# The first block's attention with transposed scores, a row-maximum pass and the softmax's sums out of the value product

## The reference, cut to what matters

```
# kind 0, window: tokens within 128 positions, all 256 context tokens, and a sink logit per head
s_loc = einsum(q, k) * 64**-0.5, masked where |qpos - kpos| > 128
s_ctx = einsum(q, k_ctx) * 64**-0.5
p = softmax(concat[s_loc, s_ctx, sink])          # the sink takes weight, but has no value
o = p_loc @ v + p_ctx @ v_ctx
# kind 1, global: 512 tokens and 256 context tokens
p = softmax(einsum(q, [k, k_ctx]) * 64**-0.5);  o = p @ [v, v_ctx]
# layer 0 only: the 256 context queries, over the 256 context keys, both kinds (kind 0 with the sink)
```

## Time and profile before

| | |
|---|---|
| median of 3 runs | 3906.89 us (3906.81 to 3909.35) |
| the profiled execution's own time | 3902.73 us |
| its span | 3900.9 us |
| TensorE busy | 3302.3 us, 85% |
| VectorE busy | 1055.7 us, 27% |
| ScalarE busy | 659.3 us, 17% |
| GpSimd busy | 440.3 us, 11% |
| mean granted clock of TensorE | 0.86 |

### The profile page before, as it was taken

The page is one execution under the profiler, slowest core; times in us unless marked ns, Lnnn a source line. Parts: engine busy times, 40 slices in busy tenths (PEclk is TensorE's granted clock), DMA queues, the critical chain, the costliest instruction groups (busy, mean ns, idle before and its releaser), DMA issues. The chain is left out here.

```text
span 3900.9 us, 41076 instructions
## 1 busy us (share of the span) xinstructions
PE 3302.3 (85%) x16972; PEld 1921.7 (49%) x16972; DVE 1055.7 (27%) x2000; ACT 659.3 (17%) x1275; POOL 440.3 (11%) x636
## 2 busy tenths in 40 slices
PE   3799998479999938999758777479998998879997
PEld 0456773323333303577332111168785586748875
DVE  0225542321111122443130000132324266222232
ACT  0111120100000111111100000032222155122231
POOL 1006700011111110170001111100000000000000
PEclk7896558589999968855869999889999979989998
DMA  9131000369999891100249999912312100132130
GB/s 393 39 97 44 1 0 11 140 234 389 385 388 391 308 374 54 65 1 1 78 172 413 414 412 412 371 54 87 108 58 97 65 1 1 65 113 87 65 119 27
DMA packets 141428, 637.02 MB, mean 163 GB/s; under 512 B 11824, under 2 KB 19008, under 8 KB 86000
## 3 DMA queue, kind: packets, MB, share of 16 engines
q1 hardware_dynamic: 121104, 575.58, 37.4%
q0 software_dynamic: 20192, 59.58, 5.0%
HBM read 611.95 MB, written 23.17 MB: 163 GB/s over the span
## 5 line engine op out<-in xcount | busy, mean ns | idle before, releaser
L897 PE MATMUL bank<-slots,HT 128*32 128x512 f32 x4096 | 479.1, 600 | 79.3 <-DMA slots<-in_w_up_dram 41.5
L667 PE MATMUL bank<-slots,HT 128*128 128x512 f32 (+2 forms) x960 | 400.7, 578 | 20.4 <-ACT done_mark L1531 20.4
L897 PEld LDWEIGHTS bank<-slots,HT 128*32 128x32 f32 x4096 | 121.7, 110 | 400.8 <-issue 243.4
L667 PEld LDWEIGHTS bank<-slots,HT 128*128 128x128 f32 x960 | 182.4, 192 | 230.3 <-issue 204.5
L667 PE MATMUL bank<-hT_high,chunk_high 128*128 128x512 f32 x704 | 277.3, 394 | 8.3 <-DVE low_slots L1922 8.3
L667 PE MATMUL bank<-hT_high,low_slots 128*128 128x512 f32 x704 | 277.7, 395 | 0.0
L667 PE MATMUL bank<-hT_low,chunk_high 128*128 128x512 f32 x704 | 276.9, 393 | 0.0
L916 PE MATMUL bank<-arena,HT 128*32 128x512 f32 x2048 | 243.9, 596 | 26.7 <-DMA arena<-in_w_down_dram 26.2
L698 PE MATMUL bank<-ident,arena 128*128 128x128 f32 x272 | 61.0, 402 | 223.0 <-DVE arena L1593 145.5
L667 PE MATMUL bank<-HT,slots 128*128 128x512 f32 (+1 forms) x480 | 172.3, 521 | 1.7 <-ACT done_mark L1531 1.7
L698 PEld LDWEIGHTS bank<-ident,arena 128*128 128x128 f32 x272 | 50.2, 212 | 237.5 <-issue 198.8
(11 more groups left out here) (323 smaller groups left out, 4431.0 us busy)
## 6 DMA issues: line engine op xcount, KB each, us to landing
slots<-in_w_gate_dram SPq DMA_DIRECT2D x128, 1024.0 KB, 8.6
slots<-in_w_up_dram SPq DMA_DIRECT2D x128, 1024.0 KB, 11.0
arena<-in_w_down_dram SPq DMA_DIRECT2D x128, 1024.0 KB, 13.2
slots<-in_ada_w_dram SPq DMA_DIRECT2D x24, 2048.0 KB, 22.2
slots<-in_w_in_dram SPq DMA_DIRECT2D x15, 2048.0 KB, 13.0
slots<-in_ffn_w_gate_dram SPq DMA_DIRECT2D x10, 2048.0 KB, 8.5
slots<-in_ffn_w_up_dram SPq DMA_DIRECT2D x10, 2048.0 KB, 8.8
slots<-in_ffn_w_down_dram SPq DMA_DIRECT2D x10, 2048.0 KB, 7.8
```

Of the source, the lines that this page charges most:

```text
L667: mm = pe.matmul(out_, lhsT, rhs, start=(n == 0), stop=(n == len(pairs) - 1))
L897: mm = pe.matmul(bank[32 * j:32 * j + 32, 2 + n, :], xT[:, kk0 + kk, lo:lo + 32], w[n][:, kk, 512 * h:512 * h + 512], start=(pair == 0 and ...
```

## The change

A group now is a pair of query heads (they share a key/value head) with either all 512 token queries (a main group) or all 256 context queries. Layer 0 has eight groups: four of context queries (kind 1 twice, kind 0 twice), then four main groups in the same order. Layer 1 has the four main ones.

1. Row pass. For every group the old scores (queries in rows) are computed first, only to find each row's maximum: `row_scores` writes them to banks 4 and 5, `maximum` reduces them. There is one pair of banks, so each unit waits for the reduce of the unit before it. The negative maxima are transposed into one row (`turn_shift`) and copied by ACT (`take_shift`) to partition 64 of the queries (`Q_ext`), against which the keys (`K_ext`) have a row of ones.
2. Key loop. Per key tile and head, keys (stationary, 65 rows) times up to 512 queries (moving) give scores with keys in rows and the maximum already subtracted; ACT takes the exponential of 512 columns into `probT`; PE multiplies 128 columns of values and ones (`V_ext`, stationary) with it. One half of the result's partitions holds the output, the other the sum of the weights. No probabilities and no outputs are transposed. For kind 0 the sink's exponential enters as one more product.
3. Outcome. DVE takes the reciprocal of the sums (64 partitions x 512) and multiplies, straight into `HT`.
4. The row pass of a group is issued inside the key loop of the group two before it (layer 0) or one before it (layer 1), shared out over its steps but the last; the first two groups (or one) have theirs at the stage's start.
5. In `qkv` ACT writes each key/value head's queries and keys apart (eight copies per tile for two) and the values in two copies. GpSimd fills the rows and columns of ones and zeros.
6. `Q_ext` lies in the two weight slots of `w_out`. SP loads `w_out`, and all that follows it in its queue, after the stage's last mix.
7. DVE takes over the 31-tap convolution's first half for the context tokens from GpSimd: 93 taps for 62 in layer 0, two after each unit of the row pass.

```diff
+def attention_plan(layer):
+    kinds = [(kind, g) for kind in (1, 0) for g in range(2)]
+    order = ([(kind, g, False) for kind, g in kinds] if layer == 0 else []) + [(kind, g, True) for kind, g in kinds]
+    groups, units, steps, events = [], 0, 0, 0
...
+    b = 2 * (step.number % 2) + (j or 0)
+    step.parts.append((j, b, events, last.get(b)))
+    last[b] = events
...
+        def Q_ext(layer):
+            return mixer_slots(layer)[:, 0:2 * HEADS * NTOK].rearrange("p (a h n) -> p a h n", a=2, h=HEADS)
...
+    if stage.name == "attend":
+        attended = stage.at("mixed", stage.signals["mixed"])
+    if stage.name == "w_out":
+        sp.wait_ge(sem["mixed"], attended)
...
+    def row_scores(unit):
+        group, qt = unit.group, unit.qt
+        if unit.number:
+            pe.wait_ge(sem["rowmax_free"], st.at("rowmax_free", unit.number))
+        if unit is group.units[0] and group.number:
...
+        q = q_ext[0:HD + 1, group.kind, group.heads + unit.j, tile_cols(qt)]
...
+        pe.matmul(bank[:, 5, 0:CTX], q, kT[:, SEQ:NTOK], start=True, stop=True).then_inc(sem["rowmax_full"], 1)
...
+    def turn_shift(group):
+        pe.wait_ge(sem["neg_max"], st.at("neg_max", group.number + 1))
+        n = len(group.tiles)
+        for j in range(2):
+            for i in range(n):
+                c = 16 + 8 * (group.number % 2) + j * n + i
+                mm = pe.transpose(bank[0:1, 4 + j, tile_cols(i)], small[:, c:c + 1], ident[:, :])
+        mm.then_inc(sem["shift_full"], 1)
...
+    def scores(one):
+        group = one.group
+        if one.first:
+            pe.wait_ge(sem["shift_done"], st.at("shift_done", group.number + 1))
+        keys = K_ext[0:HD + 1, group.kind, group.g, tile_cols(one.kt)]
+        for j, b, event, previous in one.parts:
+            if previous is not None:
...
+            edges = []
+            if group.kind == 0 and one.kt < ST:
+                edges = [(t, 0 if t < one.kt else 1) for t in (one.kt - 1, one.kt + 1) if 0 <= t < ST]
+            mm = pe.matmul(bank[:, b, 0:one.hi - one.lo], keys, q_ext[0:HD + 1, group.kind, group.heads + j, one.lo:one.hi],
+                           start=True, stop=not edges)
+            for t, side in edges:
+                lo = P * t - one.lo
+                mm = pe.matmul(bank[:, b, lo:lo + P], ident[:, :], band[:, side, :], start=False, stop=t == edges[-1][0])
+            mm.then_inc(sem["score_full"], 1)
...
+            if one.first and group.number:
+                pe.wait_ge(sem["mixed_taken"], st.at("mixed_taken", 2 * group.number - 1 + j))
+            p = probT[:, b, 0:hi - lo] if group.main else probT[:, b, CTX * j:CTX * j + CTX]
+            at_v = P * group.g + HD * (1 - j)
+            mm = pe.matmul(bank[:, 6 + j, lo:hi], V_ext[:, one.kt, group.kind, at_v:at_v + P], p,
+                           start=one.first, stop=ends)
...
+        if group.kind == 0 and one.last:
+            pe.wait_ge(sem["sink_row"], st.at("sink_row", 2 * sum(other.kind == 0 for other in groups[:group.number + 1])))
+            rows = sink_rows(st.layer, sum(other.kind == 0 for other in groups[:group.number]))
+            for j in range(2):
+                pe.matmul(bank[:, 6 + j, 0:n], sink_sel[0:HD + 1, HD * j:HD * j + P], rows[0:HD + 1, j, 0:n],
+                          start=False, stop=True).then_inc(sem["mixed"], 1)
...
+    for group in groups:
+        later = groups[group.number + ahead] if group.number + ahead < len(groups) else None
+        units = list(later.units) if later else []
+        share = -(-len(units) // (len(group.steps) - 1))
+        for n, one in enumerate(group.steps):
+            if n + 1 < len(group.steps):
+                scores(group.steps[n + 1])
+                for unit in units[share * n:share * n + share]:
+                    row_scores(unit)
+            else:
+                if later:
+                    turn_shift(later)
+                if group.number + 1 < len(groups):
+                    scores(groups[group.number + 1].steps[0])
+            mix(one)
...
+            turned = bank[:, b, 0:3 * P].rearrange("p (k n) -> p k n", n=P)
+            for g in range(2):
+                rows = slice(HD * g, HD * g + HD)
+                if not keys_only:
+                    act.activation(q_ext[0:HD, kind, 2 * g:2 * g + 2, tile_cols(i)], turned[rows, 0:2, :], ACT.Copy)
+                ins = act.activation(K_ext[0:HD, kind, g, tile_cols(i)], turned[rows, 2, :], ACT.Copy)
+            ins.then_inc(sem[f"free{b}"], 1)
...
+        act.wait_ge(sem["shift_full"], st.at("shift_full", group.number + 1))
+        if group.kind == 0:
...
+            for j in range(2):
+                act.activation(rows[HD:HD + 1, j, 0:n], bank[0:1, 4 + j, 0:n], ACT.Exp, scale=HD ** -0.5,
+                               bias=sink[0:1, st.layer, group.heads + j:group.heads + j + 1]).then_inc(sem["sink_row"], 1)
+        act.activation(q_ext[HD:HD + 1, group.kind, group.heads:group.heads + 2, group.queries[0]:group.queries[1]],
+                       bank[0:1, 4:6, 0:n], ACT.Copy).then_inc(sem["shift_done"], 1)
...
+            act.wait_ge(sem["score_full"], st.at("score_full", event + 1))
+            wait_read(previous)
+            n = one.hi - one.lo if one.group.main else SEQ
+            act.activation(probT[:, b, 0:n], bank[:, b, 0:n], ACT.Exp, scale=HD ** -0.5).then_inc(sem["prob_ready"], 1)
...
+            ins = dve.tensor_reduce(small[:, c:c + 1], flat_bank[:, 5 * BANK - keys:5 * BANK + CTX], AX.X, ALU.max)
...
+        ins.then_inc(sem["rowmax_free"], 1)
...
+    def outcome(group):
+        n = group.queries[1] - group.queries[0]
+        cols = slice(*group.queries)
+        for j in range(2):
+            y, total = slice(HD * j, HD * j + HD), slice(HD * (1 - j), HD * (1 - j) + HD)
+            dve.wait_ge(sem["mixed"], st.at("mixed", 2 * group.number + 1 + j))
+            step(dve.reciprocal(one_over[y, 0:n], bank[total, 6 + j, 0:n]))
+            dve.tensor_tensor(HT[y, 4 + 2 * group.kind + group.g, cols], bank[y, 6 + j, 0:n], one_over[y, 0:n], ALU.mult)\
+               .then_inc(sem["mixed_taken"], 1)
...
+    ready_taps = itertools.chain.from_iterable(zip(*([taps(1, 0), taps(1, 1), taps(0, 1)] if l == 0 else [taps(1, 0)])))
...
+    for group in groups:
+        if group.number + ahead < len(groups):
+            for unit in groups[group.number + ahead].units:
+                maximum(unit)
+                tap_some(2)
+        else:
+            tap_some(16)
+        outcome(group)
+    tap_some(3 * TAPS_B)
...
-                (0, conv_b_in, conv_b_w, TAPS_B, PAD_B, HT[:, 2, lo:hi])):
+                (0, conv_b_in, conv_b_w, TAPS_B, PAD_B, HT[:, 2, lo:hi]))[:3 - part]:
...
+    step(pool.memset(K_ext[HD:HD + 1, :, :, :], 1.0))
+    step(pool.memset(Q_ext(st.layer)[HD:HD + 1, :, :, :], 0.0))
+    for c in range(0, 5, 2):
+        step.later(pool.memset(V_ext[:, :, :, HD * c:HD * c + HD], 1.0))
+    step(pool.memset(sink_sel[0:HD + 1, :], 0.0))
+    for turn in range(2):
+        step(pool.memset(sink_rows(st.layer, turn)[0:HD, :, :], 0.0))
+    step(pool.memset(sink_sel[HD:HD + 1, HD:2 * HD], 1.0))
```

More of the change, by code:

```diff
@@ L118, in place_stages, with __init__ @@
     return total
[L121 to L134, removed]
+class Group:
+    def __init__(self, number, kind, g, main):
+        self.number, self.kind, self.g, self.main = number, kind, g, main
+        self.queries = (0, SEQ) if main else (SEQ, NTOK)
+        self.heads = 2 * g
+        self.tiles = list(range(ST)) if main else list(range(ST, ST + CT))
+        self.keys = list(range(ST, ST + CT)) + (list(range(ST)) if main else [])
+        self.units, self.steps = [], []
@@ L739, in attend @@
             def attend(st):
[L740 to L753, removed]
+                groups = st.facts["groups"]
@@ L1215, in take_turned @@
                     keys_only = st.layer == 1 and i >= ST
[L1216 removed]
+                    q_ext = Q_ext(st.layer)
                     for kind in range(2):
@@ new lines, in attend @@
+                for group in groups:
+                    for one in group.steps:
+                        for j, b, event, previous in one.parts:
+                            if one.last and group.kind == 1:
+                                mixed += 1 if group.main else 2
+                                mixes[event] = mixed
+                            else:
+                                read += 1
+                                reads[event] = read
+                    if group.kind == 0:
+                        mixed += 2
@@ new lines, in wait_read @@
+                def wait_read(event):
+                    if event in mixes:
+                        act.wait_ge(sem["mixed"], st.at("mixed", mixes[event]))
+                    elif event is not None:
+                        act.wait_ge(sem["prob_read"], st.at("prob_read", reads[event]))
+                ahead = 2 if st.layer == 0 else 1
+                for group in groups[:ahead]:
```

(7 more changed lines are left out.)

299 lines of the change are left out of this document (153 added, 146 removed).

## The result

Median 3945.3 us (3942.7 to 3951.4, 4 runs) against 3907.3 (3906.8 to 3909.4, 4 runs) before on the same chip: ratio 1.0099, 95% interval 1.0081 to 1.0116. The kernel became 38 us slower. The forecast was 3926 (+19.5), range 3884 to 3962. The direction held, and the time lies in the range, but only half of the loss was forecast. The next lines also show that the half that was forecast didn't come from where it was put.

The account below looks back on a forecast made before the run. Both attentions were taken as bound by TensorE's own instructions, at half clock. Layer 0 +18.7, layer 1 -2.2 and qkv +3.0 gave +19.5 us on 3906.9, so 3926 us, range 3884 to 3962.

Parts of the forecast that it names:

- layer 1's start: Layer 1's attention before its key loop: eight row units, negation, transposes and a copy, 35.4 us.
- context part: Layer 0's start and four context-query groups, all at half clock: 125.3 us.
- main part: Layer 0's fifth to eighth groups with last outcome and handover, at full clock: 146.4 us.
- lag: Key loop's first steps before full clock is granted: 3 us lost in layer 0, 6 in layer 1.
- the clock's fall behind three boundaries: Between main groups, waits drop the clock: 5 us at half after each, 2.5 lost, 7.5 per layer.
- 128-column product: Band matmuls of windowed groups: 0.67 us each at half clock, 0.33 at full, twelve bands 4.0 us.
- the first rival: 65 rows act like 96 and the clock holds through the row units: 33 us less, 3893 us; chance 0.20.
- the second: Rival: the clock holds over the boundaries between groups: 15 us less, 3911 us; chance 0.14.
- The fourth: Rival: 65-row scores keep the clock at 0.50 in the main groups too: 4115 us; chance 0.05.
- The third: Rival: without transposes, full clock also in both starts: 22 us under the first rival, 3871 us; chance 0.08.
- The boundaries: Between groups, TensorE waits for outcomes: reciprocals of 3.3 us, TensorE idle 3.5 to 5 us at six boundaries.
- the queue behind `w_out`: SP's loads of w_out and later weights, now after the last mix: zero; without cover up to 17 us a layer.

Follow-up runs that it names:

- e2: The changed kernel, with GpSimd in layer 1 waiting for its last sum before issuing the next tap's product: 3897.9 us, ratio 0.9978.
- e5: The changed kernel, with two of VectorE's convolution taps behind each of the eight reduces at layer 1's start: 3900.0 us, ratio 0.9983.
- e7: e2 with 128 rows for 65 in all score products, the row pass too: 3866.2 us, ratio 0.9892.
- e10: e7 with two pairs of banks for the row scores at both layers' starts: 3846.0 us, ratio 0.9843.
- e1: The changed kernel, with the negative maxima computed one column at a time: 3930.0 us, ratio 1.0063.
- e8: e10 with ScalarE copying out the mixed banks, and one reciprocal and product for both heads behind the next group's second reduce: 3808.5 us, ratio 0.9748.
- e11: e8 with 65 rows again for 128 in all score products: 3844.9 us, ratio 0.9842.

## Why the prediction was wrong, and what of it held

**The step that failed** is layer 1's start, "7 x 4.0 + 2.97, negation, transposes, a copy: 35.4". The wait of the negation for GpSimd was put at nothing: the negation had been costed like its one-column predecessor, and lasted 48.5 us, more than the 42.3 us by which layer 1's attention grew. All else in that start came as written: eight units at 3.98, reduce 0.96, TensorE idle 1.05 before each, clock 0.50. Without the negation's 48.5 layer 1's attention would be 215, and e2 and e5 measure 215.9 and 216.0; forecast 219.1. The trace of before held a hint: the prediction itself put a tap at 1 us beside GpSimd, and used that as a price only, without asking what else such contention touches. The change widened a small instruction from one column to four, and took the taps out of the start, where VectorE had met GpSimd all the time before. A duration was carried over to a form that had no row and got no bounds.

**That the time lies in the range is luck.** Two errors of opposite sign met, 48.5 us forgotten and some 22 put too much.

**Layer 0 was 17 us too dear.** Its context part took 120.5 us for 125.3, the main part 144.4 for 146.4. The fifth to eighth groups and the end measured 39.1, 44.4, 27.0, 25.4 and 8.4 us, from reciprocal to reciprocal, where 41.5, 44.9, 26.1, 26.1 and 7.8 were forecast. On top the forecast put 3 us of lag and 7.5 us for the clock's fall behind three boundaries, and the measured groups hold these already. The clock did fall as forecast: behind the last wait of each boundary TensorE works 6.7, 4.0 and 4.2 us at half clock, 15 us as put.

So the groups' own terms were too high. One of them is the 128-column product, put at 0.33 us at full clock as half of the 0.67 read from the earlier trace rows; at full clock it takes 0.22 to 0.23 (a band starts at 506.73 us, the next product at 506.96), 1.3 us less for twelve bands, and a pair of windowed row units with its reduce takes 4.3 us (506.51 to 510.80) where 4.1 + 0.84 were put, four times in each of two groups. That is some 8 of the 12.5 us that the forecast was too high in the main part; the rest is open. In the context part the clock was at full for some 14 of the 120.5 us (mean 0.56), where 0.50 was put throughout; how much of the 4.8 us this is worth no run shows.

In layer 1 the lag was real: the first group takes 48.8 us from its first scores to its reciprocal for 40.6 put, and the other three and the end hold 1.6 us of the 7.5 put for boundaries, 4 us too much in all. So the forecast was 17.3 + 4.0 + 0.7 us too high in the parts it knew, and would have to be -2.5; without the negation's wait the change measures -8 us (e2), between the times of the first rival (3893) and the second (3911), by neither's mechanism. The 5 us between -2.5 and -8 are open.

**The clock** went as forecast: 0.56 in layer 0's first 120 us, 0.89 behind. The forecast's reason was waits between the row units; e7 shows that 65 rows share in it, and e10 that the waits do too. The first rival (65 rows act like 96 and the clock holds through the row units) is refuted: it needs 1.00 there, and with 65 rows the eight units of layer 1's start all ran at 0.50. The fourth (0.50 in the main groups) is refuted by 0.89. The third, that transposes alone had held the clock down, is refuted a second time: the context part has hardly any and stays at 0.56.

**The boundaries** came as forecast: TensorE waits 5.33, 1.68 + 3.02 and 1.69 + 3.02 us at the three between layer 0's main groups, and the reciprocals take 3.36 us, 3.35 in the earlier trace rows.

**Costed at nothing, and nothing:** the queue behind `w_out` (its first matmul comes 21.8 us behind attention, 21.9; in layer 1 15.1 for 16.2), though the load now lies in that stretch, at a DMA share of 0.70 (the last of the windows above); GpSimd's fills, 12.3 us in layer 1's `qkv`; ScalarE's exponentials, which end no wait of TensorE in the key loop. These hold.

## What to carry to other kernels

Before a small VectorE instruction is widened, or moved to a place where VectorE is otherwise quiet, ask which of its forms share ports with GpSimd and whether GpSimd ever pauses there: a GpSimd sequence without a pause is harmless by its busy time and can hold a 0.15 us instruction, and all that waits for it, until its end. A pause of 0.08 us per pair (e2), single columns (e1), or regular turns between the two engines (e5) cure it; the second only for the instruction that has it. And where the clock's fall is priced, price only the matmuls in it, not the waits: in e8 against e11, 102 us less of half clock gave 33 us.

## What the runs showed of the hardware

- A two-port VectorE instruction (four columns, or 512, from SBUF to SBUF) waited 34.5 to 48.5 us, through as many as 44 GpSimd instructions of 1.0 to 1.3 us each. The Trainium skill ("SBUF — State Buffer", "Who interferes with whom") says that whoever issues first gets the shared pair for the whole instruction and the other blocks. By that the wait would end with the GpSimd instruction under way, after at most 1.3 us. In taking turns that is what the traces show (a negation lasts 1.31 us at most in e2 and e5); behind 13.8 us or more of undisturbed sequence it isn't.
- Taps with two SBUF inputs, in turns with GpSimd, lasted up to 1.83 us (e7, e10) for 0.73 alone; none of them waited longer, none behind more than 10.7 us of undisturbed sequence.
- Score products over the same columns in the same order were granted 0.74 with 65 rows and 0.85 with 128 (layer 0), 0.77 and 0.89 (layer 1); the added rows are zeros in the queries and add nothing to the sums, and they count all the same. An instruction costs the same time with either at the same clock (the 512-column one of a row unit 1.87 us from start to start at half clock with 65 rows and with 128).
